# One-hot marks of product-key experts: both halves by VectorE for four tokens at once, the gate by ScalarE, row dots and gathers shifted

## The reference

```python
    gate = jax.nn.softmax(best_s, axis=-1)
    act = jax.nn.gelu(jnp.einsum('td,thkd->thk', h, expert_u[expert_idx]).astype(jnp.float32),
                      approximate=False)
    coef = (gate * act).astype(h.dtype)
    return jnp.einsum('thk,thkd->td', coef, expert_v[expert_idx])
```

## Time and profile before

| what | value |
|---|---|
| median of 3 runs | 2115.41 us (2114.46 to 2116.15) |
| profiled execution | 2107.43 us |
| its span | 2105.6 us |
| mean granted TensorE clock | 0.993 |
| TensorE / VectorE / ScalarE / GpSimd busy | 97% / 74% / 39% / 45% |
| DMA | 470.11 MB, mean 223 GB/s |

### The profile page before, as it was taken

One profiled execution on the slowest core, in us unless ns is written; L12 is line 12 of the kernel. 1 busy time (PEld: TensorE's weight loads), 2 busy tenths in 40 slices (PEclk: granted clock), 3 DMA queues, 4 the chain that ended last, 5 costly groups with the idle time before them and its releaser, 6 DMA issues.

```text
span 2105.6 us, 39943 instructions
## 1 busy us (share of the span) xinstructions
PE 2036.1 (97%) x13974; PEld 1795.8 (85%) x13974; DVE 1556.5 (74%) x3582; ACT 814.7 (39%) x1303; POOL 957.0 (45%) x585
## 2 busy tenths in 40 slices
PE   5899999999999998999999999999999999999997
PEld 2788888888787887889999999999988888888886
DVE  5777777777541117779889889889559988888888
ACT  3544444444343234333443433434333333333332
POOL 0413344223334447445899856666773322222222
PEclk9899999999999999999999999999999999999999
DMA  7323222222213345434698869989999999999993
GB/s 272 107 78 105 80 85 94 91 79 104 81 44 116 111 145 183 123 102 144 229 291 266 281 231 342 331 321 329 361 403 400 372 376 355 368 343 360 350 359 120
DMA packets 151787, 470.11 MB, mean 223 GB/s; under 512 B 15632, under 2 KB 46576, under 8 KB 148464
## 3 DMA queue, kind: packets, MB, share of 16 engines
q1 hardware_dynamic: 108064, 300.13, 41.7%
q0 software_dynamic: 36864, 134.23, 17.3%
q10 hardware_dynamic: 6736, 34.08, 4.1%
HBM read 415.38 MB, written 53.00 MB: 222 GB/s over the span
## 4 chain that ended last, share of the span: by engine, by line
PE 80%; DVE 7%; DMA 5%; POOL 4%; issue 2%; ACT 1%; SPq 1%; ACTq 0%; DVEq 0%; POOLq 0%
PE bank L2902 23%; PE bank L589 12%; PE bank L591 12%; PE bank L590 12%; POOL w_lo L1265 3%; DMA rows<-peer_u,e_row 3%; PE bank L2888 3%; PE pair L589 2%; PE bank L2495 1%; PE bank L2485 1%; PE pair L590 1%; PE pair L591 1%; DVE rows L2059 1%; PE bank L2317 1%; PE bank L2458 1%
## 5 line engine op out<-in xcount | busy, mean ns | idle before, releaser
L1265 POOL TENSOR_TENSOR w_lo<-raw,w_hi 128x1024 fp32r<-128x1024 f32 x148 | 363.1, 2454 | 501.9 <-ACT w_hi L789 269.5
L589 PE MATMUL bank<-lat_hi,w_hi 128*128 128x384 f32 (+2 forms) x1488 | 536.6, 361 | 8.8 <-ACT gl L1117 4.6
L591 PE MATMUL bank<-lat_hi,w_lo 128*128 128x384 f32 (+2 forms) x1488 | 521.8, 351 | 0.0
L590 PE MATMUL bank<-lat_lo,w_hi 128*128 128x384 f32 (+2 forms) x1488 | 521.2, 350 | 0.0
L589 PEld LDWEIGHTS bank<-lat_hi,w_hi 128*128 128x128 f32 x1488 | 281.0, 189 | 24.2 <-issue 10.0
L591 PEld LDWEIGHTS bank<-lat_hi,w_lo 128*128 128x128 f32 x1488 | 280.6, 189 | 17.9
L590 PEld LDWEIGHTS bank<-lat_lo,w_hi 128*128 128x128 f32 x1488 | 281.4, 189 | 13.4 <-issue 0.2
L1385 POOL DMA_INDIRECT rows<-peer_v,e_row x128 | 136.5, 1066 | 337.2 <-DVE pair L2201 313.2
L1265 POOL TENSOR_TENSOR w_lo<-raw_more,w_hi 128x1024 fp32r<-128x1024 f32 x80 | 200.2, 2505 | 107.7 <-ACT w_hi L1014 55.2
L2902 PE MATMUL bank<-w_hi,c_hi 128*128 128x512 f32 x768 | 237.4, 389 | 0.6 <-DVE w_lo L2189 0.6
L2902 PE MATMUL bank<-w_lo,c_hi 128*128 128x512 f32 x768 | 237.2, 389 | 0.0
(11 more groups left out here) (397 smaller groups left out, 3540.1 us busy)
## 6 DMA issues: line engine op xcount, KB each, us to landing
raw<-w SPq DMA_DIRECT2D x210, 512.0 KB
raw_more<-w SPq DMA_DIRECT2D x142, 512.0 KB
g_dram<-gs ACTq DMA_DIRECT2D x24, 1024.0 KB
gu_dram<-gu SPq DMA_DIRECT2D x120, 192.0 KB
gq<-g_dram SPq DMA_DIRECT2D x45, 512.0 KB
gl<-gu_dram SPq DMA_DIRECT2D x28, 768.0 KB
ada<-w_ada SPq DMA_DIRECT2D x32, 512.0 KB, 4.2
dY<-gc_dram SPq DMA_DIRECT2D x8, 768.0 KB, 4.2
```

Of the source, the lines that this page charges most:

```text
L589: nc.tensor.matmul(out, hi, rh, start=start, stop=False)
L590: nc.tensor.matmul(out, hi, rl, start=False, stop=False)
L591: return nc.tensor.matmul(out, lo, rh, start=False, stop=stop)
L1265: nc.gpsimd.tensor_sub(w_lo[:, slot, :], raw_at(slot % 2 if src is None else src), w_hi[:, slot, :].bitcast(F32)).then_inc(split_done, 1)
```

## The change

- `marks` makes both one-hots with one comparison of 128x512 each, `hole_j` first, both without the gate.
- ScalarE multiplies `hole_j` in place with the gate of each token (`gate_marks`, four operations of 128x128 a group), two groups ahead of TensorE; the first two groups in front of the stage.
- Seven row dots per eight groups (`DOT_T`), so 84 of them in the stage, 33 before it, 11 behind it; all stand in front of the first coefficients.
- The gathers of the stage stand two tiles sooner in GpSimd's order, those of the candidates no later than there.
- TensorE computes a pair's U tile in front of its groups.
- The loops over token blocks 2 and 3 on ScalarE and VectorE are written out.

```diff
--- before.py
+++ after.py
@@ -66,7 +66,7 @@
 X_END = X_G + DT // 8
 ROWS = 8
 DOT_CD = 11
-DOT_T = 6
+DOT_T = 7
 DOT_G = (LAT - 1) * DOT_CD
 DOT_END = DOT_G + DOT_T * (DT // 32)
 V_BANK = ((0, 1), (4, 5), (6, 7))
@@ -1166,6 +1166,14 @@
                     act.wait_ge(g_ev, i * (2 * GTOK // 4) + (j + 1) * (GTOK // 4))
                 act.dma_start(g_dram[i * 2 + j, :, own, :], gs[:, j, own, :]).then_inc(gs_st[j], 16)
 
+            def gate_marks(g):
+
+                act.wait_ge(oh_i_done, 2 * g + 1)
+                for v in range(4):
+                    mark_ = hole_j[:, 4 * (g % 2) + v, 0:P]
+                    last = nc.scalar.activation(mark_, mark_, ACT.Copy, scale=eidT[:, 2, 4 * g + v:4 * g + v + 1])
+                last.then_inc(oh_j_done, 1)
+
             def gate_block(i, j, first):
 
                 act.wait_ge(gs_st[j], i * (16 * G_PARTS))
@@ -1174,6 +1182,9 @@
                         act.wait_ge(g_mm, i * (2 * GTOK // 4) + (j * GTOK // 4 + 2 * w + z + 1))
                         nc.scalar.copy(gs[:, j, :, 8 * w + 4 * z:8 * w + 4 * z + 4],
                                        bank[z][:, :].rearrange("p (t i) -> p i t", t=4)).then_inc(g_ev, 1)
+                    for g in range(2 * (8 * (2 * i + j) + w + 1), 2 * (8 * (2 * i + j) + w + 2)):
+                        if g < DT // 4:
+                            gate_marks(g)
                     x = X_G + j * (GTOK // 8) + w
                     act.wait_ge(a_mm, i * (2 * GTOK // 8) + (x + 1))
                     act.wait_ge(gu_st[x % 4], i * (4 * GTOK // 4 // 2) * 2 + x // 4 * 16 + 16)
@@ -1184,11 +1195,12 @@
                     if w in G_STORE and not (first and j == 0):
                         store_g(i if j else i - 1, 1 - j, G_STORE.index(w))
 
-            for j in range(2):
-                gate_block(0, j, True)
-            with act.Fori(1, DT // GTOK // 2) as i:
+            act.wait_ge(e_free, LAT)
+            for g in range(2):
+                gate_marks(g)
+            for i in range(DT // GTOK // 2):
                 for j in range(2):
-                    gate_block(i, j, False)
+                    gate_block(i, j, i == 0)
 
             def act_c(i, y):
 
@@ -1393,9 +1405,9 @@
                 if q < ROWS:
                     return u + X_CD + U_CD[0] - 3 + q // 2
                 if n < DOT_G:
-                    return u + X_CD + U_CD[0] + 2 + n * U_CD[1] // DOT_CD
+                    return u + min(X_CD + U_CD[0] + 2 + n * U_CD[1] // DOT_CD, X_G - 2)
                 if n < DOT_END:
-                    return u + X_G + (n - DOT_G) * 4 // DOT_T
+                    return u + X_G - 2 + (n - DOT_G) * 4 // DOT_T
                 if n < P:
                     return u + X_END + (n - DOT_END) * (PK - X_END) // (P - DOT_END)
                 return T_V + n - P + RING + 1
@@ -2053,11 +2065,12 @@
 
             def dot(i, q):
 
+                q += i * (4 * DOT_T)
                 if q % 2 == 0:
-                    dve.wait_ge(row_in[q % ROWS // 2], i * (4 * DOT_T * 4) + (q // ROWS + 1) * 32)
+                    dve.wait_ge(row_in[q % ROWS // 2], (q // ROWS + 1) * 32)
                 row = rows[:, q % ROWS, :]
                 nc.vector.scalar_tensor_tensor(row, row, 1.0, pair[:, :], ALU.mult, ALU.mult,
-                                               accum_out=e_dot[:, bass.ds(i * (4 * DOT_T) + q, 1)]).then_inc(row_used, 1)
+                                               accum_out=e_dot[:, q:q + 1]).then_inc(row_used, 1)
 
             def candidates(b):
 
@@ -2138,12 +2151,9 @@
                 z = g % 2
                 own = slice(4 * z, 4 * z + 4)
                 cols = bass.ds(i * 128 + 4 * g, 4)
-                nc.vector.tensor_tensor(hole_i[:, own, 0:P], rep(bank[5][:, 0:P], 4), bc(eidT[:, 0, cols], P),
-                                        ALU.is_equal).then_inc(oh_i_done, 1)
-                for v in range(4):
-                    col = bass.ds(i * 128 + (4 * g + v), 1)
-                    nc.vector.tensor_scalar(hole_j[:, 4 * z + v, 0:P], bank[5][:, 0:P], eidT[:, 1, col], eidT[:, 2, col],
-                                            ALU.is_equal, ALU.mult).then_inc(oh_j_done, 1)
+                for hole, half_ in ((hole_j, 1), (hole_i, 0)):
+                    nc.vector.tensor_tensor(hole[:, own, 0:P], rep(bank[5][:, 0:P], 4), bc(eidT[:, half_, cols], P),
+                                            ALU.is_equal).then_inc(oh_i_done, 1)
 
             def token_block(i, first):
 
@@ -2157,9 +2167,9 @@
             dve.wait_ge(e_free, 2)
             token_block(0, True)
             dve.wait_ge(e_free, LAT)
-            with dve.Fori(1, DT // P) as i:
+            for i in range(1, DT // P):
                 token_block(i, False)
-            for q in range(DOT_END, P - 4):
+            for q in range(DOT_END, P):
                 dot(0, q)
 
             def coefficients(i, x, first=False):
@@ -2206,8 +2216,6 @@
             for x in range(4):
                 low_parts(0, x)
                 coefficients(0, x + 2, True)
-            for q in range(P - 4, P):
-                dot(0, q)
             for x in range(4, 16):
                 low_parts(0, x)
                 coefficients((x + 2) // 16, (x + 2) % 16, x < 14)
@@ -2879,16 +2887,16 @@
 
             with pe.Fori(0, DT // 32) as i:
                 for w in range(4):
+                    pe_u(i * 4, X_G + w)
                     for z in range(2):
-                        pe.wait_ge(oh_i_done, i * 8 + (2 * w + z + 1))
-                        pe.wait_ge(oh_j_done, i * 32 + (8 * w + 4 * z + 4))
+                        pe.wait_ge(oh_i_done, i * 16 + 2 * (2 * w + z + 1))
+                        pe.wait_ge(oh_j_done, i * 8 + (2 * w + z + 1))
                         if z == 0:
                             pe.wait_ge(g_ev, i * 8 + 2 * w)
                         for v in range(4):
                             last = mm(bank[z][:, v * P:(v + 1) * P], hole_j[:, 4 * z + v, 0:P], hole_i[:, 4 * z + v, 0:P],
                                       start=True, stop=True)
                         last.then_inc(g_mm, 1)
-                    pe_u(i * 4, X_G + w)
             for x in range(X_END, PK):
                 pe_u(0, x)
 
```

## The result

The changed kernel takes 2092.62 us (median of four runs, 2091.04 to 2094.03) against 2114.93 us of the kernel before (four runs, 2106.03 to 2116.15): 0.9904 of the time, interval 0.9885 to 0.9924, so some 20 us (16 to 24 by the interval) faster. A repeat in another comparison gave 2092.66 us and 0.9907 (0.9886 to 0.9927).

A forecast was written before the change was run, and what follows sets the result against it. TensorE was taken as the bound, busy 2036.1 of 2105.6 us, so only idle time could be won. Group stage 5.5, tail 4.1 and clock 1.7 made 11.3 us, off the median 2115.4: 2104.1, range 2101.0 to 2113.

The forecast's parts named there:

- Group stage: TensorE's waits in the groups: 7.6 us idle less 1.3, 0.3 and 0.5 kept, so 5.5 us won.
- other late rows: Group stage: 0.5 us of TensorE's idle time kept for rows that still come late.
- the stall at rows 38 and 39: First pair of rows of the group stage, gathers not moved two tiles: 1.3 us of TensorE's idle time kept.
- Tail: Behind the groups: 5.1 us idle less 1.0 kept, so 4.1 won; 1.7 more as the clock does not fall.
- the load of `gq`: Tail: next in line, issued behind the last store of g; 1.0 of the 5.1 us kept for it.
- not a gain on top: Turn of VectorE's block loop, 3.44 us standing: TensorE's loss behind it counted as part of the 6.9 us waits.
- entry: Start of the group stage: the U tile in front, 4.16 us, just covers ScalarE's first products; 0.3 us allowed.
- all that can be won 14.4 us: Whole gain possible: 7.6 idle in groups, 5.1 idle in tail, 1.7 of low clock; 0.7% of the span.
- The tail keeps its stalls: Rival: tail stalls hang on SP's wait for the last store of g and on gq; 2109.5 us, chance 0.17.
- The waits change place: Rival: TensorE waits for ScalarE's products where it waited for hole_j; within 4 us of 2115, chance 0.09.
- DMA engines bound: Rival, group stage: at 340 GB/s a pair takes 6.36 us; 2121 us in all, chance 0.08.
- VectorE's 1.0 us of new room per pair: Group stage: cheaper one-hots bring VectorE's pair to 4.4 us, leaving 1.5 us of room instead of 0.5.

The follow-up runs named there:

- the loop alone: Kernel before with VectorE's second and third token block written out, nothing else: 2108.59 us, 0.9987.
- sooner gathers alone: Kernel before with the gathers of the group stage two tiles sooner, nothing else: 2099.97 us, 0.9952.
- Gathers at their old places: Changed kernel with the group stage's gathers at their old place in GpSimd's order, still seven dots per eight groups: 2171.72 us, 1.0265.
- the gate alone: Changed kernel with six dots, old gather places, U tile behind its groups and four dots behind the fourth coefficients again: 2119.35 us, 1.0042.
- the core of the change: Kernel before with seven dots, sooner gathers, VectorE's blocks written out, all dots before the coefficients; gate on VectorE, U tile behind: 2093.03 us, 0.9914.
- U tile behind: Changed kernel with each U tile behind its two groups, as before the change: 2098.56 us, 0.9924.
- the fourth profile of before: Kernel before, unchanged, profiled once more to find an execution of its upper level: 2113.07 us.

## Why the prediction was right or wrong

**The sum was too small, in four terms.**

- *Group stage: 5.5 forecast, 8.5 in the traces.* The step that failed is the first one of the prediction, where stalls were sized by the idle time that the rows record: 7.6 us. The pairs lost 10.5. A record of a matmul is 0.28 or 0.33 us long, while the next one starts 0.11 or 0.17 us later in a running stream; in front of a wait the record's end hides some of it. Ten waits at about 0.27 us more each, and one distance that is 0.17 longer with no idle time recorded, are the 2.9. The reserve of 0.5 for other late rows wasn't needed; the stall at rows 38 and 39 took 1.70 where 1.3 was kept.
- *Tail: 4.1 + 1.7 forecast, 6.7 measured.* The reserve of 1.0 us for the load of `gq` wasn't needed: idle time is nought and ScalarE's `c_hi` waits for no coefficient.
- *V stage: nothing forecast, 1.5 measured.* It is TensorE's waits for `w_lo` in the kernel before, 0.6 us recorded and 1.1 by the two distances that hold them, and 0.4 in three distances with no idle time recorded.
- *The difference was taken off the median.* The sum was made from a profiled execution of 2107.4 us and taken off 2115.4, as if the 8 us between them lay outside the change. The experiments' profiles of before lose up to 3.4 us more in the groups, much of it at the turn of the loop, which had been costed at "not a gain on top". That holds for the first profile (2.0 us lost there) and not for all (up to 6.2). The changed kernel has no such place, and its nine runs lie within 5 us (2089.9 to 2094.0), where those of before spread over 6 to 13 in the comparisons. The turn alone taken out gave 2.4 us (the loop alone, at the edge of what can be told). How the remaining 4 us of the 20 divide stays open: no profile of before is as slow as its median of 2115.

In one sum: the time is 11.5 us below the forecast of 2104.1. 5.1 of that is the traces' 16.4 against the sum's 11.3 (groups 3.0, tail 0.9, V stage 1.5, entry -0.6, 0.3 unplaced); 6.4 is that the profiled execution stood 8.0 us under the median of before and only 1.6 under that of after.

With "all that can be won 14.4 us" as the low end of the range, all of this but the tail lay outside it (5.1 + 1.7 had been counted there, 6.7 came). A bound on a gain that is made from recorded idle time is no bound.

**The mechanisms held.** Late rows held up the groups: with sooner gathers alone nearly all of it goes. The tail's stall came by coefficients behind dots: ScalarE's wait for them is gone, and the clock stays at 1.00. ScalarE had room for 384 products, first late pair and entry were as worked out.

**The rivals.** *The tail keeps its stalls* is refuted, 62.5 us for 62.4 of work. *The waits change place*: only for rows 38 and 39. *DMA engines bound*: refuted over 100 us in which 366 GB/s are moved with TensorE always busy. The Trainium skill (Perfetto Trace Analysis, Engine Utilization) gives a core 358 GB/s of memory bandwidth, and some 120% of that as the practical ceiling when the other core of its pair is idle; the windows with 389 GB/s and the earlier trace rows with 408 lie between the two. What the neighbour did isn't recorded. But slower than before was near in a way that no rival named: by the loop of late gathers. *Gathers at their old places* shows its price with the gate on ScalarE, 60 us over the kernel before, with the DMA engines at three quarters.

**What the forecast could not see: which part carries.** It gave VectorE's 1.0 us of new room per pair a central place. In the runs sooner gathers bring 12 us; seven dots, all in front, with the loop written out 7 more; one comparison per one-hot, the gate on ScalarE and the U tile in front nothing: the kernel with none of these three takes 2093.0 us. So the term that the forecast argued longest, VectorE's room and ScalarE's cover for it, carried none of the gain, and the right direction came from the gathers and the dots. The parts don't add up. With the gate on ScalarE, seven dots without sooner gathers cost 60 us, six dots all in front give back the 18, seven with four behind give back 10.

## What to carry to other kernels

When a stall goes through several in-order queues, follow the chain until it comes back to its own start: a lap longer than the work it has to cover makes every round late, and one more step of lead time is worth more than a faster engine in the lap. Size a stall by the distance between starts on the bound engine against an undisturbed stretch, not by the recorded idle time. Before a sum is taken off a median, see where the profiled execution stands among the runs; where it is the fastest, look for what varies.

## What the runs showed of the hardware

- A wait of TensorE costs some 0.27 us more than its recorded idle time (10.3 us of longer distances with 7.6 us recorded in ten waits).
- The lower clock came behind shorter stalls than the earlier trace rows had it: 2.03 us idle (two waits) and then 0.66, 2.78 us idle and then a mean of 0.72; behind a single wait of 1.70 us in the changed kernel it stayed at 1.00. The length of the stall doesn't decide it here: 1.85 us (the gate alone) and 2.52 us (the core of the change) were followed by the lower level, 2.85 us (U tile behind) and 2.90 us (the fourth profile of before, in two waits like the 2.78 us) were not.
- The turn of a loop cost VectorE 2.7 to 4.9 us without work, different in each execution, and TensorE 1.3 to 6.2.
- The mix of weight tiles, stores and gathers of 4 KB rows ran at 366 GB/s and a share of 0.98 for 100 us without a wait of TensorE.
- A gather of 128 rows of 4 KB took 5.3 to 7.3 us in the chains read here, and what stands behind it in GpSimd's queue waits for the buffer that it waits for.
